# Up projection: the third weights of a pair are rounded on GpSimd instead of ScalarE, and the pairs next to each group's end are written out

## The reference, cut to what matters

```
def encoder_layer(x, ...):                      # 2560 tokens, D_MODEL 1024, D_FF 4096
    ...                                         # input projection, Fourier and window attention heads
    x = layer_norm(ALPHA * x + heads @ w_out, ln_mix_g, ln_mix_b)
    h = jnp.square(jax.nn.relu(x @ w_ff1))      # the up projection: the change is here
    x = layer_norm(ALPHA * x + h @ w_ff2, ln_ffn_g, ln_ffn_b)
    return x
```

## Time and profile before

| | |
|---|---|
| median of 3 runs | 2411.53 us (2410.62 to 2412.11) |
| the profiled execution | 2409.59 us, of which the span is 2407.9 us |
| TensorE busy | 2356.0 us, 98% of the span |
| VectorE, ScalarE, GpSimd busy | 65%, 46%, 8% |
| granted TensorE clock, mean | 0.996 of 2.4 GHz |
| up projection, group 0 steady | windows of 40 us with 40.00 us of TensorE busy, 14.57 us from one pair to the next |
| TensorE idle from 850 to 1634 us | 784 - 773.17 = 10.8 us, all before 1346 us |

### The profile page before, as it was taken

How to read it: one execution, slowest core, us unless ns; L and a number is a source line. 1 busy time by engine, 2 the same in 40 slices (tenths; PEclk the granted TensorE clock), 3 DMA queues, 4 the chain that set the end, 5 groups by cost and what they waited for, 6 DMA issues and landing times. The chain is left out here.

```text
span 2407.9 us, 34854 instructions
## 1 busy us (share of the span) xinstructions
PE 2356.0 (98%) x12028; PEld 2058.7 (85%) x12028; DVE 1569.4 (65%) x2207; ACT 1102.3 (46%) x1820; POOL 183.8 (8%) x245
## 2 busy tenths in 40 slices
PE   7999989999999989999999999999999999999998
PEld 6888877999788889999999788888888888888887
DVE  8555366766666787786666655556566866764657
ACT  4111146887211265556556544445444444443333
POOL 2000001221223200000000000000000100000002
PEclk9999999999999999999999999999999999999999
DMA  8765776222466766677677655558877887787663
GB/s 303 281 265 229 273 212 225 77 68 88 127 229 245 282 243 245 262 267 269 239 264 266 258 205 196 211 198 309 279 225 212 271 299 226 211 277 257 194 195 118
DMA packets 220608, 547.85 MB, mean 228 GB/s; under 512 B 21704, under 2 KB 90952, under 8 KB 200908
## 3 DMA queue, kind: packets, MB, share of 16 engines
q1 hardware_dynamic: 204416, 488.19, 58.2%
q0 software_dynamic: 16080, 58.20, 7.6%
HBM read 365.95 MB, written 180.36 MB: 227 GB/s over the span
## 5 line engine op out<-in xcount | busy, mean ns | idle before, releaser
L71 PE MATMUL e_bank<-e_hi,e_lo 128*128 128x512 f32 x1120 | 435.8, 389 | 0.1
L72 PE MATMUL e_bank<-e_lo,e_hi 128*128 128x512 f32 x1120 | 435.7, 389 | 0.0
L73 PE MATMUL e_bank<-e_hi 128*128 128x512 f32 x1120 | 435.7, 389 | 0.0
L2362 DVE TENSOR_TENSOR e_lo<-e_raw,e_hi 128x896 fp32r<-128x896 f32 (+1 forms) x168 | 190.0, 1135 | 126.7 <-ACT e_hi L2317 126.5
L2317 ACT CAST e_hi<-e_raw 128x896 fp32r<-128x896 f32 (+1 forms) x168 | 165.2, 983 | 204.0 <-PE e_bank L73 198.1
L71 PEld LDWEIGHTS e_bank<-e_hi,e_lo 128*128 128x128 f32 x1120 | 210.2, 188 | 44.6 <-DVE e_lo L2362 1.0
L72 PEld LDWEIGHTS e_bank<-e_lo,e_hi 128*128 128x128 f32 x1120 | 210.2, 188 | 43.7
L73 PEld LDWEIGHTS e_bank<-e_hi 128*128 128x128 f32 x1120 | 210.2, 188 | 43.5
L71 PE MATMUL u_bank<-u_x_hi,u_wa_lo 128*128 128x384 f32 (+1 forms) x576 | 207.5, 360 | 4.1 <-ACT c_vt_raw L2060 3.9
L71 PE MATMUL u_bank<-u_x_hi,u_wb_lo 128*128 128x384 f32 (+1 forms) x576 | 203.5, 353 | 6.6 <-DVE u_x_first L1885 3.3
L73 PE MATMUL u_bank<-u_x_hi,u_wa_hi 128*128 128x384 f32 (+1 forms) x572 | 205.8, 360 | 0.0
(11 more groups left out here) (334 smaller groups left out, 4919.2 us busy)
## 6 DMA issues: line engine op xcount, KB each, us to landing
u_w_sum<-s_ws SPq DMA_DIRECT2D x33, 1024.0 KB, 4.8
c_vt_raw<-w_ff SPq DMA_DIRECT2D x24, 1024.0 KB, 7.0
c_q_raw<-w_ff SPq DMA_DIRECT2D x24, 1024.0 KB, 7.1
s_h<-c_k_raw SPq DMA_DIRECT2D x32, 768.0 KB, 6.9
e_raw<-s_t SPq DMA_DIRECT2D x96, 256.0 KB, 3.7
e_raw<-s_h SPq DMA_DIRECT2D x112, 192.0 KB, 2.8
ab_place<-w_ff SPq DMA_DIRECT2D x18, 1024.0 KB, 8.5
s_h<-c_k_raw SPq DMA_DIRECT2D x96, 192.0 KB, 2.6
```

What stands on the lines that cost most here:

```text
L71: tensor.matmul(out, w_lo, m_hi, start=first, stop=False, skip_group_check=again)
L72: tensor.matmul(out, w_hi, m_lo, start=False, stop=False, skip_group_check=again)
L73: return tensor.matmul(out, w_hi, m_hi, start=False, stop=last, skip_group_check=again)
L2362: dve.tensor_tensor(part(lo, n), part(raw, n), part(hi, n).bitcast(F32), ALU.subtract).then_inc(split, 1)
```

## The change

GpSimd's queue in the up projection becomes a body per pair. At the end of pair n it waits for `prod_done` of all seven products, then for the sums and the raw weights, and makes both roundings of `wb_high` for pair n+1. ScalarE's wait and its `wb_high(n + 1, ...)` go (it still makes pair 0's). The loads of x stand between these bodies: those with `X_FREED` None at pair 11, those freed by a product before the last in pair 15 in front of the wait for the pair's end, and the one freed by the last product (part 6 of group 2) behind the rounding. The loop covers pairs 2 to 9, and pairs 10 to 15 are written out.

```
-                with eng.Fori(1, NP // 2 - 2) as i:
+                with eng.Fori(1, NP // 2 - 3) as i:
                     for s in range(2):
                         body(g, i * 2 + s, s, False, False)
-                for p in range(NP - 4, NP - 1):
+                for p in range(NP - 6, NP - 1):
...
         @block.gpsimd
+            def wb_high(g, n, s, second):
+                if g:
+                    pool.wait_ge(w_sum_ld, (n - NP) * 16 + 48)
+                elif second:
+                    pool.wait_ge(w_sum_ld, 32)
+                else:
+                    pool.wait_ge(w_summed, n - 1)
+                pool.wait_ge(w_ld[s], (n - s) * 8 + 16)
+                pool.sem_inc(pool_passed, 1)
+                pool.tensor_copy(wb_hi[:, 1:3, :], w_sum[:, 2:4, :])
+                pool.tensor_copy(wb_hi[:, 0, :], w_raw[s][:, 2, :]).then_inc(wb_hi_done, 1)
+
+            def body(g, p, s, start, end):
+                n = g * NP + p
+                if g < LAST and isinstance(p, int) and p == NP - 5:
...
+                            load_x(g + 1, j)
+                if end and g < LAST:
+                    for j in range(NPROD):
+                        if X_FREED[g + 1][j] not in (None, NPROD - 1):
+                            load_x(g + 1, j)
+                if not (end and g == LAST):
+                    pool.wait_ge(prod_done, n * NPROD + NPROD)
+                    wb_high(g + 1 if end else g, n + 1, 1 - s, start and g == 0)
+                if end and g < LAST:
+                    for j in range(NPROD):
+                        if X_FREED[g + 1][j] == NPROD - 1:
+                            load_x(g + 1, j)
...
         @block.scalar
                 finish(n, 21, u3[:, 0:w], w)
-                if more:
-                    act.wait_ge(prod_done, n * NPROD + NPROD)
-                    wb_high(n + 1, 1 - s)
                 if near != 1:
                     finish(n, 12, u2[:, 0:w], w)
```

More of the change, by code:

```diff
@@ L1757, in mlp_up @@
         wa_hi_done, wa_split = al.sem("wa_hi_done"), al.sem("wa_split")
-        wa_second = al.sem("wa_second")
+        wa_second, pool_passed = al.sem("wa_second"), al.sem("pool_passed")
         late_quarters, late_mixed = al.sem("late_quarters"), al.sem("late_mixed")
@@ L1867, in _, with load_x @@
         def _(pool):
-            for g in range(len(UP_GROUPS)):
+            def load_x(g, j):
+                freed = X_FREED[g][j] if g else None
+                if g:
+                    pool.wait_ge(prod_done, (g * NP - 5) * NPROD if freed is None else (g * NP - 1) * NPROD + freed + 1)
                 q = first_pair(g)
[L1871 to L1878, removed]
+                pool.dma_start(x_slot(g, j, False).rearrange("p q k c -> p q (k c)"),
+                               xb_d[q:first_pair(g + 1), :, j, :].rearrange("q p c -> p q c")).then_inc(x_ld[j], 16)
@@ new lines, in body @@
+            def body(g, p, s, start, end):
+                n = g * NP + p
+                if g < LAST and isinstance(p, int) and p == NP - 5:
+                    if g == 0:
+                        pool.wait_ge(mix_st[1], 16 * (NT // 4))
+                    for j in range(NPROD):
+                        if X_FREED[g + 1][j] is None:
+                            load_x(g + 1, j)
[7 more added lines that the diff above has]
+                if end and g < LAST:
+                    for j in range(NPROD):
+                        if X_FREED[g + 1][j] == NPROD - 1:
+                            load_x(g + 1, j)
@@ L1880, in _ @@
+            pool.wait_ge(mix_st[0], 16 * (NT // 4))
+            for j in range(X_FIRST, NPROD):
+                load_x(0, j)
+            pairs(pool, body)
         @block.vector
```

## The result

The kernel after takes 2416.35 us (median of 21 runs), the kernel before beside it 2412.35 us (21 runs). One run of each took far longer (10153.7 and 4923.4 us) and is left out of the ranges, 2413.7 to 2420.3 and 2409.6 to 2415.5 us, and of the ratio. The ratio of the two is 1.0021, with a 95% interval of 1.0015 to 1.0027: +5.1 us (+3.6 to +6.5), while the medians differ by 4.0 us. The forecast was +4.4 us and 2415.9 us. The profiled execution of after took 2416.11 us, 6.52 us more than that of before. These two aren't an even pair: the profile of after lies at the median of its runs, that of before (2409.59 us, mean granted clock 0.996) lies about 2 to 3 us under the medians of before, whose runs have a mean clock of 0.994.

A forecast was written before the change was run, and what follows sets the result against it. TensorE was taken to bound the up projection, with idle time only in the first pairs and at the two group boundaries. Terms 1.3 + 1.1 + 0.2 + 0.5 + 1.3 = 4.4 us took the median from 2411.5 to 2415.9 us; range 2410.5 to 2421.

The forecast's parts named there:

- The bound, and what could be won: Up projection: TensorE sets the time, steady pairs cost 0; at most the 3.9 us copy wait of P1 can be won.
- GpSimd's price: Each pair's rounding on GpSimd: 1.04 us plus 0.55 us, together 1.55 us, starting 0.1 us after VectorE's line 1986.
- The margin of 0.8 us: Steady pairs of group 0: lateness VectorE can absorb, 0.5 us in front of u2 and 0.3 in front of P3.
- Two engines at one port: GpSimd's rounding and VectorE operations with two SBUF inputs take turns; wb_low 1.2 us late in pairs 13 and 14, group 0.
- Pair 2, +1.1: Group 0, pair 2: no margin behind the late mix, so the delay passes on to P3, +1.1 us.
- Boundary 0/1, +0.5: Between groups 0 and 1: w_sum load 1.2 us later, roundings of 1.46 us gone; middle of -0.26 and +1.2, +0.5 us.
- Group 1, +0.2: Pairs 14 and 15 of group 1: x_low of 2048 columns but no w_sums, so more VectorE idle time, +0.2 us.
- Boundary 1/2, +1.3: Between groups 1 and 2: P3's chain gains 0.6 us, a low-clock stretch moves behind P3 for 1.9 us, +1.3 us.
- No taking of turns: Rival, 12%: a rounding slows nothing on VectorE, so the delays go; 2409.7 to 2411.6 us.
- All copy waits won: Rival, 3%, at the boundaries: the 3.9 us of copy waits and 1.9 us of low clock are won; 2405.7 us.
- Clock at one more place: Rival, 17%: clock also falls at P3 of the first boundary or pair 2, 1.5 to 1.9 us each; 2417.5 to 2420.
- GpSimd late in every pair: Rival, 8%: GpSimd's late start uses up the margins in the 12 pairs of group 0 with w_sums, 4.8 us; 2421 us.

The follow-up runs named there:

- e5: Kernel after with two more GpSimd roundings of 128x400 per pair, into a tile nothing reads: 2427.25 us (4 runs), 1.0064 to the kernel before.
- e2: Kernel after, but ScalarE rounds in the six pairs where VectorE has a split of x or the late mix beside it: 2411.61 us, 0.9993 to before.
- e1: Kernel after with GpSimd's roundings given back to ScalarE, written-out pairs and moved loads of x kept: 2413.38 us, 1.0003 to the kernel before.
- e3: Kernel after with 12 idle matmuls of 512 columns before P3 in the first pair of group 2: 2414.13 us, 1.0008 to the kernel before.
- e4: Kernel after, GpSimd rounding the parts for P4 and P7 once P4 is done, the third after P3: 2413.42 us, 1.0003 to the kernel before.
- e6: e2 with 8 and 12 idle matmuls before P3 in the first pairs of groups 1 and 2: 2408.81 us, 0.9987 to the kernel before.
- e8: Kernel before, ScalarE rounding everywhere, with e7's 4 and 8 idle matmuls and its later split of raw wa weights: 2411.33 us, 1.0000 to before.
- e7: e6 with 4 and 8 idle matmuls, and VectorE splitting raw wa weights behind part 6 of x in those pairs: 2406.08 us, 0.9977 to before.

## Why the prediction held, step by step

The total came out within 1 us of the forecast by either count (+4.0 and +5.1 us for +4.4). The mechanism is the one forecast, but that the sum is so near is in part luck: its terms were off by 0.1 to 0.6 us, in both directions.

**The bound, and what could be won.** Right. TensorE is at 98%, steady pairs don't see the move (VectorE's wait of 11.7 us for 11.3), and the copy of P1 went from 3.9 to 0.6 us without a gain: at both boundaries P3 took the time back.

**GpSimd's price.** Right. 1.04 us as in the earlier trace rows, and 0.61 us for the 128x512 half, where I took 0.55; the start was 0.16 to 0.23 us behind VectorE's line, 0.1 in the text. The margin of 0.8 us was 0.76 in e5.

**Two engines at one port.** Right in kind and size. The delay of wb_low in pair 14 was 1.18 us (1.2 predicted), by x_low of 2.33 us and a rounding of 2.14 us, and e2 takes it away by moving the rounding of six pairs back. The Trainium skill (GPSIMD Engine Reference, section Key points) names VectorE operations with two SBUF inputs as the ones that clash. The trace agrees, and shows the other side too: beside line 2020 with a PSUM input the roundings took 1.05 and 0.62 us.

**Pair 2, +1.1.** Mis-sized: 0.82 us. I let nearly the whole rounding pass on. The first two of the four operations of the late mix took 1.27 and 0.94 us instead of 0.68 and 0.69, the second rounding 1.07 us instead of 0.61, and wb_low came 0.83 us late where it is 1.18 us in pair 14. That part of the rounding fitted between the operations is likely, and e5's 0.11 us fits it, but it wasn't tried alone.

**Boundary 0/1, +0.5.** Mis-sized: 0.86 us, within the bounds of -0.26 and +1.2. P1 came 2.23 us later, not 1.2. Timeline of after:
```profile
1089.01 1.05 ACT L2061 CAST u_wa_hi<-u_w_sum 128x1024 fp32r<-128x1024 f32 x1 [4.60 <-DMA u_w_sum<-s_ws]
...
1090.08 1.81 DVE L1950 TENSOR_TENSOR u_wa_lo<-u_w_sum,u_wa_hi 128x1024 fp32r<-128x1024 f32 x1 [3.30 <-ACT u_wa_hi L2061]
...
1089.79 1.03 POOL L1886 CAST u_wb_hi<-u_w_sum 128x1024 fp32r<-128x1024 f32 x1 [5.38 <-PE u_bank L73]
1090.76 1.60 POOL L1887 CAST u_wb_hi<-c_vt_raw 128x512 fp32r<-128x512 f32 x1
...
1091.95 0.44 PE L71 MATMUL u_bank<-u_x_hi,u_wa_lo 128*128 128x384 f32 x1 [2.37 <-DVE u_wa_lo L1950]
```

The load of `w_sum` is late (4.60 us of wait for it, 3.85 in the earlier trace rows), as predicted. But GpSimd waits for the same sums, and starts 0.78 us after ScalarE's rounding of the other half, so VectorE's subtraction for P1 has both roundings beside it and takes 1.81 us instead of 1.22. I had not looked for a second place where the two meet in one boundary. The parts of the 2.2 us are 1.18 us of late issue of the load, 0.46 us by which the load itself takes longer to ScalarE's rounding (8.72 us for 8.26; e1 and e2 have some 0.4 us there without GpSimd's rounding in pair 15) and the 0.58 us of the clash. P2 then gave back 1.74 us, of which 1.46 is the wait for the copy.

**Group 1, +0.2.** Mis-sized: 0.47 us. 0.15 us of it comes from what I had put down at nothing, the loads of x. GpSimd issues two of them after the rounding for pair 11, at 1256.50 us, and SyncE's load of `w_sum` follows at 1258.51; before it was 1250.83 and 1253.94. ScalarE's wait for that load went from 2.70 to 3.58 us. In e1, where no rounding stands in front of these loads, the wait for `w_sum` is 2.37 us and P1 of pair 12 isn't late; in e2 it is 3.60 us again. So the place of the loads behind the rounding is the cause; that the two transfers then share the engines is likely, but not shown. e5 shows how near this place is to costing much: +2.2 us there.

**Pair 1, -0.35.** Not in the sum. ScalarE's copy of P1 comes earlier here as well, 1.42 us against the stage's start.

**Boundary 1/2, +1.3.** The sum was near (1.62 us), but two errors lie in its parts. The chain up to P3 was to gain 0.6 us and lost 0.04. The step that failed is that the load of part 6 would land as before: GpSimd issues it behind its rounding, at 1330.40 us instead of 1323.54, 6.86 us later where the load in front is 4.76 us later (1326.26 against 1321.50), and ScalarE's rounding of the part, at 1342.45 against 1337.01, is 5.44 us later in a stage that was 4.90 us late by then. Those 0.54 us are the gain that is missing. In e1, where no rounding stands in front of the load, the part is rounded at 1341.74 and the loads are 4.43 us late, so 0.30 of the 0.54 us may be chance. The low clock cost 1.58 us for 1.9, and e3 confirms 1.6 to 1.8 us. But e1 shows the same fall with ScalarE rounding, so it is only in part an effect of the change. How large a part stays open; without any of it this profile would show +3.2 us. The mean granted clock of all runs, 0.9937 in 20 of after and 0.9941 to 0.9946 in the three groups of before beside the experiments, makes it likely that some is: a difference of 0.0004 to 0.0009 is 2 to 4 us more at the lower level, and costs half of that at most (an estimate).

**The rivals.** No taking of turns: excluded by the row of 2.14 us and by e2. All copy waits won: the waits went, P3 took it. Clock at one more place: not in after (1.00 behind the waits of 2.37 us at P1 and of 2.14 us at P3), but in e1, e4 and e5, so the chance was real. GpSimd late in every pair: e5 made it so, at 0.92 us of delay, and the price was +11 us.

## What to carry to other kernels

In these runs an operation moved to GpSimd costs just its own duration where VectorE runs nothing with two SBUF inputs beside it; where it does, add both durations, and look for every such meeting along the path, not only at the one that the change aims at. Before a wait is removed, find the wait behind it that the same stretch ends in: by products e6, which shortens the waits for the copy, is 2.1 us ahead of before, e8, which shortens those of P3, 0.2 us, and e7, with both, 4.2 us. A stretch of low clock that is hidden in a later wait is a cost in store, and a few idle matmuls in the wait in front of it take it away (e3, e6); where the wait is shorter than they are, they are a cost themselves (e8).

## What the runs showed of the hardware

- GpSimd rounds 128x512 f32 to fp32r in 0.61 us and 128x1024 in 1.04 us, within 0.01 us of ScalarE for the larger form. Two of 128x400 took 0.98 us.
- Beside a VectorE operation with two SBUF inputs both are stretched: up to 2.67 us for GpSimd's 0.61 us form, x_low from 1.75 to 2.33 us, a subtraction of 128x1024 from 1.22 to 1.81 us. The tile's view of `u_wb_hi` on GpSimd (min/median/max ns):
```profile
L1886 POOL CAST u_wb_hi<-u_w_sum x47: 1034/1043/1638, 867.9 to 1621.7; 128x1024 fp32r<-128x1024 f32 x47
...
L1887 POOL CAST u_wb_hi<-c_vt_raw x23: 613/616/2670, 883.6 to 1603.6; 128x512 fp32r<-128x512 f32 x23
```

- The granted clock fell to the 1.2 GHz level behind waits of 2.47 us (before), 3.69 us (after), 3.84 us (e2), 2.10 us (e1) and 1.85 us (e5), and stayed up behind 2.14 and 2.37 us (after) and behind 3.00 us (e1). The length of the one wait in front doesn't decide it.
